# Prompt attention in pairs of heads: logits and scores in two row groups, values transposed in two column halves

## The reference, cut to what matters

```python
I[t, s] = sum_h w[t, h] * relu(iq[t, h] . ik[s] / 8)       # indexer, 8 heads of width 64, one shared key
keep    = the 128 causally admissible keys of t with the largest I[t, s]
S_h     = q_h . k_h / 8 + (0 where kept, -1e30 elsewhere)  # 8 query heads, 4 key/value heads, width 64
o_h     = softmax(S_h) @ v_h                               # goes on as the transposed branch (channels x tokens)
```

## Time and profile before

| what | us |
|---|---|
| median of 3 runs | 3721.38 |
| lowest, highest | 3715.35, 3735.82 |
| span of the profiled execution | 3705.2 |
| PE busy in it | 3389.1 (91%) |
| DVE busy | 1756.2 (47%) |
| ACT busy | 750.4 (20%) |
| POOL busy | 261.9 (7%) |

### The profile page before, as it was taken

How to read it: one execution, slowest core, us unless ns; L and a number is a source line. 1 busy time by engine, 2 the same in 40 slices (tenths; PEclk the granted TensorE clock), 3 DMA queues, 4 the chain that set the end, 5 groups by cost and what they waited for, 6 DMA issues and landing times. The chain is left out here.

```text
span 3705.2 us, 45255 instructions
## 1 busy us (share of the span) xinstructions
PE 3389.1 (91%) x18070; PEld 2392.7 (65%) x18070; DVE 1756.2 (47%) x3303; ACT 750.4 (20%) x1584; POOL 261.9 (7%) x266
## 2 busy tenths in 40 slices
PE   5999899999888889999989998998998988999998
PEld 2644555577667767888846445455766676778887
DVE  2145487134544555455412563950445364554543
ACT  1122323112322211000012233231223231110000
POOL 0000321200100010000000004112000001000000
PEclk9999999989999999999989999997999999999999
DMA  3221255532314122222232114546341321322221
GB/s 125 72 83 70 81 181 184 173 117 103 110 42 135 41 95 69 91 69 74 74 98 97 56 58 150 169 133 212 98 132 58 101 69 36 118 69 91 78 73 67
DMA packets 274973, 366.11 MB, mean 99 GB/s; under 512 B 39262, under 2 KB 171230, under 8 KB 274628
## 3 DMA queue, kind: packets, MB, share of 16 engines
q1 hardware_dynamic: 232348, 260.85, 21.4%
q0 software_dynamic: 21504, 75.51, 6.2%
q10 hardware_dynamic: 20904, 26.78, 2.0%
HBM read 312.76 MB, written 50.34 MB: 98 GB/s over the span
## 5 line engine op out<-in xcount | busy, mean ns | idle before, releaser
L378 PE MATMUL ps<-hT,ring 128*128 128x272 f32 x3072 | 779.8, 408 | 59.8 <-PEq L155 32.3
L378 PEld LDWEIGHTS ps<-hT,ring 128*128 128x128 f32 x3072 | 589.4, 197 | 207.0 <-issue 56.9
L372 PE MATMUL ps<-ring,hT 128*128 128x512 f32 (+3 forms) x1600 | 644.1, 542 | 33.0 <-DVE hT L625 18.4
L372 PEld LDWEIGHTS ps<-ring,hT 128*128 128x128 f32 (+1 forms) x1600 | 273.2, 195 | 314.6 <-issue 292.9
L378 PE MATMUL ps<-branchT,ring 128*128 128x272 f32 x1024 | 266.9, 415 | 38.7 <-DVE arena L488 23.8
L2511 PE MATMUL ps<-hT,ring 128*128 128x272 f32 x1136 | 279.1, 396 | 17.4 <-DVE hT L2636 17.4
L378 PEld LDWEIGHTS ps<-branchT,ring 128*128 128x128 f32 x1024 | 198.8, 199 | 97.7 <-DVE arena L488 29.6
L2511 PEld LDWEIGHTS ps<-hT,ring 128*128 128x128 f32 x1136 | 217.9, 192 | 63.6 <-issue 18.2
L2511 PE MATMUL ps<-arena,ring 128*128 128x272 f32 x720 | 178.1, 402 | 13.4 <-PEq L155 10.6
L2511 PEld LDWEIGHTS ps<-arena,ring 128*128 128x128 f32 x720 | 140.0, 195 | 44.6 <-issue 11.4
L949 DVE MAX8 branchT<-arena 32x8 f32<-32x2080 f32 x64 | 148.2, 2316 | 2.2
(11 more groups left out here) (482 smaller groups left out, 4418.8 us busy)
## 6 DMA issues: line engine op xcount, KB each, us to landing
ring<-in_w_in SPq DMA_DIRECT2D x44, 2048.0 KB, 8.3
ring<-in_w_gu SPq DMA_DIRECT2D x44, 1024.0 KB, 6.5
spill<-stage ACTq DMA_DIRECT2D x72, 256.0 KB
arena<-spill SPq DMA_DIRECT2D x16, 1024.0 KB, 5.6
ring<-in_w_branch SPq DMA_DIRECT2D x16, 1024.0 KB, 5.2
ring<-in_w_down SPq DMA_DIRECT2D x8, 1536.0 KB, 6.7
ring<-in_w_down SPq DMA_DIRECT2D x8, 1280.0 KB, 5.8
ring<-in_w_out SPq DMA_DIRECT2D x4, 2048.0 KB, 9.4
```

Of the source, the lines that this page charges most:

```text
L372: mm = pe.matmul(bank[0:m, 0:w], hT[:, c, t0:t0 + m], slot3(j)[:, c, 0:w], start=(c == 0), stop=(c == kn - 1))
L378: mm = pe.matmul(bank[:, 0:HALF], slot3(j)[:, c, at:at + P], src, start=(c == 0), stop=(c == kn - 1))
```

## The change

Logits: the two heads of a pair, which lie in rows 0 to 63 and 64 to 127, are issued next to each other, into banks 0 and 1 or 2 and 3, with one fill point for each pair. Scores: the same, always into banks 0 and 1, so that scores(hp + 1) waits until both heads of pair hp are biased. Normalisation: VectorE takes the reciprocal after Exp and scales the whole row of probabilities in SBUF (`att_normed`), before the transposes. Values: V is stationary (64 columns), `PT` moves (128 columns), the two heads of a pair go to the lower and upper 64 partitions of one bank, so that the output is already channels x tokens; `on`, its transposes and their waits are gone, and ScalarE copies bank 4 + i % 2 to `brT`. The weights of the fill points of a tile sum to the same as before: 4 of 2, the large one, 12 of 1.5.

```diff
-            on = ar.take(2, 512)
...
-                weights += [1] * 8 + [(1, 35, 44, 53)[i]] + [1] * 18
+                weights += [2] * 4 + [(1, 35, 44, 53)[i]] + [1.5] * 12
...
-                        for h in range(8):
-                            n = i * 8 + h
-                            r = (h % 2) * 64
-                            if n >= 2:
-                                pe.wait_ge(S("idx_relu"), n - 1)
-                            if h < 2 and i:
-                                pe.wait_ge(S("att_biased"), 8 * i)
-                            pe.matmul(ps[n % 2][:, 0:L], iqT[r:r + 64, h // 2, q0:q0 + P], ikT[r:r + 64, 0:L]).then_inc(S("idx_logits"), 1)
+                        for hp in range(4):
+                            if hp >= 2:
+                                pe.wait_ge(S("idx_relu"), 8 * i + 2 * hp - 2)
+                            elif i:
+                                pe.wait_ge(S("att_biased" if hp == 0 else "probT_taken"), 8 * i)
+                            for u in range(2):
+                                r = u * 64
+                                pe.matmul(ps[hp % 2 * 2 + u][:, 0:L], iqT[r:r + 64, hp, q0:q0 + P], ikT[r:r + 64, 0:L]).then_inc(S("idx_logits"), 1)
...
-                        def scores(h):
-                            n = i * 8 + h
-                            r = (h % 2) * 64
-                            if h < 2:
+                        def scores(hp):
+
+                            if hp == 0:
                                 pe.wait_ge(S("idx_relu"), 8 * i + 8)
-                            if n >= 2:
-                                pe.wait_ge(S("att_biased"), n - 1)
-                            pe.matmul(ps[n % 2][:, 0:L], qT[r:r + 64, h // 2, q0:q0 + P], k2T[r:r + 64, h // 2, 0:L]).then_inc(S("att_scores"), 1)
+                            else:
+                                pe.wait_ge(S("att_biased"), 8 * i + 2 * hp)
+                            for u in range(2):
+                                r = u * 64
+                                pe.matmul(ps[u][:, 0:L], qT[r:r + 64, hp, q0:q0 + P], k2T[r:r + 64, hp, 0:L]).then_inc(S("att_scores"), 1)
 
                         def turn_probs(h):
                             n = i * 8 + h
                             if n >= 2:
                                 pe.wait_ge(S("probT_taken"), n - 1)
-                            pe.wait_ge(S("att_probs"), n + 1)
+                            pe.wait_ge(S("att_normed"), n + 1)
                             for s in range(i + 1):
                                 mm = pe.transpose(ps[2 + n % 2][:, s * P:s * P + P], Pr[:, n % 2, s * P:s * P + P], ident)
                             mm.then_inc(S("probT_ready"), 1)
 
-                        def values(h):
-                            n = i * 8 + h
-                            pe.wait_ge(S("probT_taken"), n + 1)
-                            if n >= 2:
-                                pe.wait_ge(S("att_out"), n - 1)
-                            if h == 1 and i:
-                                pe.wait_ge(S("att_turn_taken"), i)
+                        def values(hp):
+
+                            pe.wait_ge(S("probT_taken"), i * 8 + 2 * hp + 2)
+                            if hp == 0 and i >= 2:
+                                pe.wait_ge(S("att_out_taken"), i - 1)
                             for s in range(i + 1):
-                                mm = pe.matmul(ps[4 + n % 2][:, h * 64:h * 64 + 64], PT[:, n % 2, s * P:s * P + P],
-                                               vn[:, s, (h // 2) * 64:(h // 2) * 64 + 64], start=(s == 0), stop=(s == i))
+                                for u in range(2):
+                                    mm = pe.matmul(ps[4 + i % 2][u * 64:u * 64 + 64, hp * P:hp * P + P], vn[:, s, hp * 64:hp * 64 + 64],
+                                                   PT[:, u, s * P:s * P + P], start=(s == 0), stop=(s == i))
                             mm.then_inc(S("att_values"), 1)
                         share.point("pe", pe)
                         scores(0)
-                        for h in range(9):
-                            if h < 7:
-                                scores(h + 1)
+                        for hp in range(4):
+                            if hp < 3:
+                                scores(hp + 1)
                             share.point("pe", pe)
-                            if h < 8:
-                                turn_probs(h)
+                            turn_probs(2 * hp)
                             share.point("pe", pe)
-                            if h >= 1:
-                                values(h - 1)
-                        pe.wait_ge(S("att_out"), 8 * i + 8)
-                        if i >= 1:
-                            pe.wait_ge(S("att_turn_taken"), i)
-                        for c in range(4):
-                            mm = pe.transpose(ps[5][:, c * P:c * P + P], on[:, i % 2, c * P:c * P + P], ident)
-                        mm.then_inc(S("att_turned"), 1)
+                            turn_probs(2 * hp + 1)
+                            share.point("pe", pe)
+                            values(hp)
...
+                        def probs(h):
+                            n = i * 8 + h
+                            act.wait_ge(S("att_max"), n + 1)
+                            if n >= 2:
+                                act.wait_ge(S("probT_ready"), n - 1)
+                            act.activation(Pr[:, n % 2, 0:L], St[:, n % 2, 0:L], ACT.Exp, bias=mx[:, n % 2, 0:1],
+                                           accum_out=sm[:, n % 2, 0:1]).then_inc(S("att_probs"), 1)
+
+                        def take_turned(h):
+                            n = i * 8 + h
+                            act.wait_ge(S("probT_ready"), n + 1)
+                            if n >= 2:
+                                act.wait_ge(S("att_values"), n // 2)
+                            act.activation(PT[:, n % 2, 0:L], ps[2 + n % 2][:, 0:L], ACT.Copy).then_inc(S("probT_taken"), 1)
+                        probs(0)
+                        for hp in range(4):
+                            probs(2 * hp + 1)
                             share.point("act", act)
...
+                            take_turned(2 * hp)
                             share.point("act", act)
...
+                            if hp < 3:
+                                probs(2 * hp + 2)
+                            take_turned(2 * hp + 1)
                             share.point("act", act)
...
+                        act.wait_ge(S("att_values"), 4 * i + 4)
+                        act.activation(brT[:, 0:4, i * P:i * P + P], ps[4 + i % 2][:, :].rearrange("p (c t) -> p c t", c=4), ACT.Copy).then_inc(S("att_out_taken"), 1)
...
-                        for h in range(10):
+                        for h in range(9):
                             n = i * 8 + h
-                            if h >= 2:
-                                dve.wait_ge(S("att_probs"), n - 1)
-                                vch.link(dve, dve.reciprocal(sm[:, n % 2, 1:2], sm[:, n % 2, 0:1]))
                             if h < 8:
                                 dve.wait_ge(S("att_scores"), n + 1)
                                 if n >= 2:
...
                                                          ALU.mult, ALU.add).then_inc(S("att_biased"), 1)
                                 dve.wait_ge(S("att_biased"), n + 1)
                                 dve.tensor_reduce(mx[:, n % 2, 0:1], St[:, n % 2, 0:L], AX, ALU.max, negate=True).then_inc(S("att_max"), 1)
-                            if h >= 2:
-                                dve.wait_ge(S("att_values"), n - 1)
-                                if h == 2 and i >= 2:
-                                    dve.wait_ge(S("att_turned"), i - 1)
-                                dve.tensor_scalar(on[:, i % 2, (h - 2) * 64:(h - 2) * 64 + 64], ps[4 + n % 2][:, (h - 2) * 64:(h - 2) * 64 + 64],
-                                                  sm[:, n % 2, 1:2], None, ALU.mult).then_inc(S("att_out"), 1)
+                            if h >= 1:
+                                dve.wait_ge(S("att_probs"), n)
+                                vch.link(dve, dve.reciprocal(sm[:, (n - 1) % 2, 1:2], sm[:, (n - 1) % 2, 0:1]))
+                                pr = Pr[:, (n - 1) % 2, 0:L]
+                                dve.tensor_scalar(pr, pr, sm[:, (n - 1) % 2, 1:2], None, ALU.mult).then_inc(S("att_normed"), 1)
```

21 lines of the change are left out of this document (4 added, 17 removed).

## The result

The changed kernel ran at 3668.4 us (median of 4, 3667.5 to 3673.8), the kernel before beside it at 3718.9 (median of 4): ratio 0.987, 95% interval 0.984 to 0.990. So the change is clear of noise, though it is only 1.3% of the kernel. The forecast was 3694, with a range from 3678 to 3713.

A forecast was written before the change was run, and what follows sets the result against it. TensorE was taken to bound the prompt attention, busy 200.1 of 211 us. Savings of 15.5 us a layer, 31 over two, less 4 for the clock gave 27: 3721.4 to 3694 us, range 3678 to 3713.

The forecast's parts named there:

- Part 1: Logits and scores: the second of a pair is free; index logits save 5.0 us a layer, scores take 4 groups, not 7.
- Part 2: Values of a pair in two overlapping column halves take 0.41, 0.63, 0.84, 1.05 us, with 0.2 us for changing array shape.
- rival A: Values: the column halves don't overlap, costing 8.5 us a layer; gain 10, 3711 us; chance 0.10.
- (a): Before scores(1): TensorE waits until both heads of pair 0 are biased, 1.1, 1.9, 1.9, 2.3 us in tiles 0 to 3.
- (b): First chunk of a projection tile, tiles 0 to 2: TensorE waits 1.0, 1.0, 1.1 us for ScalarE to empty its bank.
- (c): Tile 3: TensorE waits 2.5 us for ScalarE's Silu copy, then 2.0 us more before values(1).
- Rival C: Tiles 1 to 3: VectorE bounds them throughout; gain 9 to 13, 3710 us; chance 0.14.
- Rival D: Every new wait of 1.9 us or more drops the clock, 5 us lost each; 9 us slower, 3730 us; chance 0.07.
- The tile sums: Tiles 0 to 3 save 0.7, 2.5, 4.8, 2.5 us; with index logits' 5.0, 15.5 us a layer.
- The clock: Granted clock falls once a layer behind tile 3's new idle stretches, 2 us each; 4 us off the gain.
- The 16.2 us "outside the span": Whole kernel: the median of three runs, 3721.38 us, lies 16.2 us above the profiled span, taken as outside it.
- Rival B: Values and clock: no cost of array shape (6.4 us), no clock fall (4); gain 37, 3684 us; chance 0.19.

The follow-up runs named there:

- e3: The change with the projection chunk moved ahead of the second pair of scores, for the first pair alone: 3663.7 us.
- e8: The change with ScalarE's second copy slot of a pair moved ahead of its copy of turned probabilities: 3655.3 us.
- e9: The change with the edits of e3 and e8 together: 3646.1 us.
- e5: The kernel before with index logits alone by pairs: 3709.8 us.
- e10: The kernel before with index logits and scores by pairs, values and normalisation as before: 3693.7 us.
- e6: The kernel before with the transposed, normalised values alone, logits and scores head by head: 3781.4 us.
- e2: The changed kernel run again without edit: 3673.7 us.
- e7: The change with two matmuls whose result nobody reads between scores(0) and scores(1) of tiles 1 to 3: 3663.4 us.
- e11: The change with 6 small transposes appended to each of TensorE's tiles 1 to 3: 3672.7 us, one execution.
- e12: The change with 64 more VectorE waits a layer, all long satisfied: 3676.7 us, one execution.
- e1: The kernel before run again without edit: 3717.3 us.

## Why the prediction missed, step by step

What held. **Part 1**: all groups are x4 at 0.49 to 1.13 us where the clock is full. **Part 2**: the column halves overlap. Values of a pair hold TensorE for 0.37, 0.58, 0.81 and 1.03 us against 0.41, 0.63, 0.84 and 1.05, so rival A is out. The Trainium skill's rule that a new tiling mode drains the array (TensorEngine Tiling (Array Packing), section Tiling Modes) gives no figure; each further block of a pair adds 0.22 us, which leaves 0.15 us for the drain and for the start of the burst together, where the earlier trace rows had 0.2. No run here separates the two. **Part 3**: the scaling of 512 columns takes 0.49 us against 0.43. **Part 4**: (a) 0.97, 2.05, 1.76 and 2.16 us against 1.1, 1.9, 1.9 and 2.3; (b) 0.85, 0.64 and 1.07 against 1.0, 1.0 and 1.1; (c) 2.60 and 1.66 against 2.5 and 2.0. Rival C is out: in the first layer of the change TensorE waits for VectorE four times, each time before scores(1), and in no later pair; the 0.4 to 0.9 us waits of this kind in e3, e8 and e9 show how little slack there was. Rival D is out by its size: 18.6 us lost to the clock in the two stages against 6.8 before, 12 us more and not 40.

What failed is the sum: the gain of the stage itself was taken too small, the clock was charged to one side alone, and the stages behind stood at nothing. Sizes, in the 23.5 us between the forecast's gain of 27 and the 50.5 measured:

1. **The tile sums, and the index part, +9.6 us.** 15.5 us a layer forecast, 20.3 measured in structure. Index logits: 5.0 forecast, about 7 measured (e5: 6.9 and 7.4). Of the missing 2 us, 0.7 is the dearer chunk that goes with each of the seven groups (1.05 us in place of 0.95 by the earlier trace rows), and 0.7 a wait for a bank in tile 2 that fell from 1.07 to 0.39 us; the rest I can't place. From tile to tile: 1.2, 3.0 and 5.6 us saved where I had 0.7, 2.5 and 4.8; tile 3 is 0.7 us longer in the profile, with 4.3 us of lost clock in it, so 3.6 in structure against 2.5. In tiles 0 to 2 the waits together came out 0.2 to 0.4 us shorter than I had them, values and turns 0.02 to 0.05 us shorter each, and a chunk that stands before a turn holds TensorE 0.86 us where I had 0.95.
2. **The clock, +4 us.** I took 4 us off, and none came off the median. I charged the change for its new waits with the clock of before as it was in one execution, in which little was lost in the stage (6.8 us). Another execution of before lost 28.2 us there, and in it the clock fell behind the very 2.13 us wait of the earlier trace rows that I had set against such falls, in both layers (the second):

```profile
2154.00:2164.00 10.00, 9.49 (x26) 4.66 (x27) 3.28 (x9) 3.25 (x10) 0.00 (x0) 0.66 0.07 26
```

The clock's loss in the kernel before was a term too, and it went into the sum as zero. Between the two profiled executions the clock took 11.8 us off the gain in the two stages, and their spans are only 38 us apart; the two medians compare at a mean clock of about 0.953 each. Straight lines through time against mean clock (54 executions of before, 8 of the change) give 3716 and 3670 us at 0.954, 46 us apart. So this step is sized to some 3 us only, as the mean clock is known to 0.001.

3. **The stages behind, +7 us.** 3.6 to 3.8 us a layer, in code with no edit, and nothing in the sum. I named these stages only as a risk. No row of before could have told; its cause is open.
4. **The 16.2 us "outside the span"** moved no gain, but it was a wrong reading: 1.8 us lie outside, and the other 14 are the clock's spread between executions. Had I asked what they are, the clock would have had a range of its own, and the range of the forecast would have reached lower.

9.6 + 4 + 7 = about 21 of 23.5 us. The rest is the draw of the first series: with the 47 us over all executions these steps account for the whole. The time then is 3671 us, still below the range. **Rival B** was nearest, with a gain of 37, but not for its reasons: its price of shape was paid nearly whole (0.15 of 0.2 us), and its "no fall" was false, since the clock fell in tile 3 in both layers.

## What to carry to other kernels

Two parts of a change can each be worthless alone and pay together: here, by the waits of e10 and e6, paired scores make the idle time that the early normalisation can use, and the normalisation without them puts a whole VectorE chain between TensorE's steps. So ask of each part which other part feeds it on time. Where short waits stand close to each other on TensorE, fill the first of them or reorder the engine that causes them; the change plus two edits of a line or two gained as much again as half of the change. And before an execution's span is used as a sum, compare its mean clock with that of others of the same kernel.

## What the runs showed of the hardware

- The same wait doesn't always cost the clock. The wait of 2.60 us in tile 3 stands in both layers of six profiled executions (the change, e2, e3, e7, e11, e12), and each time the clock fell to half behind it; 2.7 to 3.1 us were lost in the next 10 us. Behind the wait of 2.16 us a fall followed within 10 us in 9 of 14 layers, behind those of 2.0 to 2.15 and of 1.76 us in 8 of 14 each, and behind the 2.13 us of the kernel before in 3 of 6 (before, e1, e5). The largest single loss, 32 us at half clock in e1, stood behind a wait of 0.98 us. In the change the clock stays up behind the waits in tiles 1 and 2 of the first layer, and falls behind the same two in the second (windows):

```profile
258.00:264.00 6.00, 3.31 (x15) 1.58 (x14) 4.74 (x15) 2.36 (x8) 0.00 (x0) 1.00 0.09 33
310.00:316.00 6.00, 3.17 (x13) 1.43 (x12) 5.15 (x12) 2.77 (x7) 0.00 (x0) 1.00 0.00 0
...
2060.00:2072.00 12.00, 9.95 (x32) 4.34 (x33) 6.04 (x20) 3.48 (x12) 0.00 (x0) 0.72 0.02 6
2114.00:2124.00 10.00, 7.17 (x33) 3.14 (x30) 5.82 (x14) 4.19 (x11) 0.00 (x0) 0.83 0.07 26
```

- Work that nobody needs, laid into such a stretch, made the kernel 8 to 10 us faster (e7).
- Two 64-column halves fed by turns with 128 columns each take 0.26 us a block of a pair (1.03 us for four blocks, 0.22 us for each further block); four 32-column groups take 0.24.
